# Low parts in two instructions, memory heads ahead, seams in another order, post norms by column halves

## The chip, the cores and the metric

One core of a Trainium2 chip runs the whole program in one launch. The metric is the device time of an execution in microseconds. The kernel before ran three times: 1194.78, 1198.9 and 1200.14 us, median 1198.9.

## What is computed

Two transformer blocks, one after the other, on 256 tokens of width 1024, all in float32. The first block: a norm, one wide projection that feeds three mixers (softmax attention with decay, a gated delta rule with convolution, stick-breaking attention), their gated sum through `w_out`, an attention to 256 memory tokens with normalised queries and keys, and a feed-forward of width 2816 with a convolution. The second block: a SwiGLU, a mixer of block attention and pooling, an attention to a second memory, and another SwiGLU, each with a norm before and after. Cut to the second block and its norm:

```python
def rmsnorm_2(x, g):
    r = lax.rsqrt(jnp.mean(x * x, axis=-1, keepdims=True) + RMS_EPS)
    return (x * r) * g
def second_block(x, mem, ...):
    x = x + 0.5 * rmsnorm_2(swiglu(rmsnorm_2(x, ffn1_pre_g), ...), ffn1_post_g)
    x = x + rmsnorm_2(mixer(rmsnorm_2(x, mix_pre_g)) @ w_out, mix_post_g)
    x = x + rmsnorm_2(attend(rmsnorm_2(x, xa_pre_g), rmsnorm_2(mem, mem_g)) @ wo, xa_post_g)
    x = x + 0.5 * rmsnorm_2(swiglu(rmsnorm_2(x, ffn2_pre_g), ...), ffn2_post_g)
```

## The kernel before, in words

**Weights in chunks.** All weights are cut into 178 chunks of 1 MB (128 partitions x 2048 columns of float32). SP fetches chunk c into `raw[c % 3]`. ScalarE rounds it to the matmul's type, the high part `whi` (step `hi`, line 1536), and VectorE subtracts, the low part `wlo` (step `lo`, line 1793). The activations are kept as a high and a low part too, and a product is three: high by high, high by low, low by high. `RING` is 3 and `LEAD` is 2: at the start of chunk c's product the parts of chunk c + 2 are put on their engines (`split`). SP's next fetch into a slot waits for that slot's `lo`, the next `hi` for the product that last read the slot.

**Kinds of chunks.** `W`, `A` and `S` give 256 output channels turned (channels on partitions), `V` gives half of the depth for 512 value channels, `O` is a branch's output, `R` gives two blocks of depth for token rows of 1024 columns. Each product is two steps, `mm(c, 0)` and `mm(c, 1)`, and, where side work is due, each of these is cut once more (`mma` is its first half, `quarter` and `hook`). For `W`, `V` and most `R` chunks the first part reads the first 1024 columns of the slot; for `A`, `O`, the last `R` chunk and the ones marked `by_token` both parts read all of it. `multiply` (from line 1170) issues the matmuls: lines 1196, 1203, 1206, 1214, 1217, 1224, 1233 and 1248 are those of the kinds.

**The planner.** `build_plan` writes the order of the steps of every engine ahead of time. It adds up rough durations (`ROUGH`) into a clock for each engine; chains of side work (delta rule, attention heads) wait in `side`, and `hook` places the next link of each where `fits` says that its input is ready in these sums, no more than `EARLY` ahead. `drain` places all that is left, one link after another, with nothing in between. `heads_of` makes the links of heads: scores `sc`, maximum `sm`, exponential `ex`, division `pn`, turn `pt` with its copy `pc`, values `pv`, the output's high part `oc` and low part `ol`. The four memory heads run in two lanes, 0 and 2, 1 and 3, with banks 4, 5 and 6, 7; queries and keys are normalised first (`hn_sq`, `hn_sum`, `hn_r`, `hn_mul`), the queries through bank 4 and the scratch of lane 0. All four waited for `mq1` and for the copy of the values `mv`.

**Seams.** A norm of x sits between two stages: squares `ns`, root `nr`, scaling `nd`, then TensorE turns x into blocks of 128 channels (`nt`, line 1262), ScalarE scales them into the high part (`nh`, 1565) and VectorE makes the low part (`nl`, 1808). Five groups of blocks go through four banks, so the fifth turn waits until the first group is read. `fill_and_turn` puts a chunk that doesn't need x under the norm, and then the turn; at `norm_xq`, `norm_ffn` and `ffn1_pre_g_2` the chunk's addition (line 2075) and the low part of the chunk after next follow behind the turn, in this order. At `mix_pre_g_2` and `xa_pre_g_2` the filling chunks are value chunks in plain `mm` calls, with their copy (line 1607) and low parts ahead of the turn.

**Post norms.** Behind the last token-row chunk of each stage of the second block (`post`): squares of the product from PSUM on ScalarE (`post1`, line 1768), product times gain on VectorE (`post0`, 2044), root (`post_r`), and x plus that times the root (`post2`, 2049), for each 128 tokens. `post0` waits for `post1`, which writes the same scratch. For `ffn2_pre_g_2` the order is by hand in `seam`: the first 128 tokens of the last two chunks are finished first, their post norm and norm run under the other tokens' products, and the turn (`nt2`, 1277), high (`nh2`, 1572) and low parts (`nl2`, 1814) are made for each 128 tokens; the first gate chunk is multiplied in the same two passes. At the very end SP writes the output in two transfers, one for each 128 tokens (line 1022).

## Time and profile before

| | |
|---|---|
| Median of three runs | 1198.9 us |
| The profiled execution | 1200.3 us |
| Its span, first to last instruction | 1198.6 us |
| Mean granted clock of TensorE | 0.992 |
| Instructions | 16754 |
| Read from HBM | 191.82 MB |

The span and every row further down are of one execution, which took 1200.3 us; 1.7 us of it lie around the span. PE is TensorE's matmuls, PEld its weight loads, DVE is VectorE, ACT ScalarE, POOL GpSimd, SPq SyncE's queue. A row of a timeline has the start in us, the length in us, engine, line and operation, what it writes <- reads with its shape, how many were merged, and in brackets the engine's idle time ahead of it with what ended it.

### The profile page before, as it was taken

How to read it: one execution, taken by the hardware profiler on the slowest of the kernel's cores; microseconds unless marked ns; L12 is line 12 of the kernel's file. 1: busy time of each engine (PE TensorE's matmuls, PEld its weight loads, DVE VectorE, ACT ScalarE, POOL GpSimd, SP SyncE). 2: the span in 40 equal slices, each digit the busy share in tenths (PEclk: the TensorE clock that was granted, in tenths of full speed). 3: DMA queues.
4: the chain of work that ended last, by engine and by line, in shares of the span. 5: the costliest groups of instructions: out<-in, count | busy, mean ns of one | idle time of the engine just before them, and what ended most of it. 6: DMA issues, size and time to landing. Idle time of an engine off the chain costs nothing.

```text
span 1198.6 us, 16754 instructions
## 1 busy us (share of the span) xinstructions
PE 1161.4 (97%) x6779; PEld 1011.5 (84%) x6779; DVE 811.4 (68%) x873; ACT 616.5 (51%) x788; POOL 82.2 (7%) x114
## 2 busy tenths in 40 slices
PE   6999999999999999999999999999999998999997
PEld 6877888888988789999888888888776887888886
DVE  5877655855778757878648777646776656777743
ACT  6656344533767655565536344436455546444432
POOL 8001200200000000000000000002700000000000
PEclk9999999999999999999999999999999998999999
DMA  7544323432655426555665565565533523665550
GB/s 252 169 158 148 106 71 106 137 109 71 214 201 170 153 86 213 178 177 181 211 206 173 179 188 198 178 208 195 182 136 111 186 83 124 208 198 186 186 200 36
DMA packets 144132, 193.95 MB, mean 162 GB/s; under 512 B 6136, under 2 KB 121208, under 8 KB 144056
## 3 DMA queue, kind: packets, MB, share of 16 engines
q1 hardware_dynamic: 142856, 188.43, 48.4%
q0 software_dynamic: 1200, 4.46, 1.0%
q8 instruction: 54, 0.88, 0.3%
q14 instruction: 22, 0.18, 0.0%
HBM read 191.82 MB, written 1.05 MB: 161 GB/s over the span
## 4 chain that ended last, share of the span: by engine, by line
PE 87%; DVE 6%; ACT 4%; issue 2%; DMA 1%; SPq 0%; ACTq 0%; DVEq 0%
PE banks L1214 24%; PE banks L1248 20%; PE banks L1196 14%; PE banks L1217 12%; PE banks L1233 4%; PE banks L1224 2%; DVE wlo L1793 2%; ACT whi L1536 2%; PE banks L1476 1%; PE banks L1307 1%; PE banks L1350 1%; PE banks L1396 1%; PE banks L1359 1%; DMA raw<-in_w_in 1%; PE banks L1436 1%
## 5 line engine op out<-in xcount | busy, mean ns | idle before, releaser
L1793 DVE TENSOR_TENSOR wlo<-raw,whi 128x2048 fp32r<-128x2048 f32 x178 | 407.4, 2293 | 180.8 <-ACT whi L1536 180.7
L1536 ACT ACTIVATE whi<-raw 128x2048 fp32r<-128x2048 f32 x178 | 339.2, 1910 | 174.4 <-PE banks L1248 87.4
L1214 PE MATMUL banks<-xhl,whi 128*128 128x512 f32 x1232 | 399.1, 405 | 3.4 <-DVE fq_ L2075 1.6
L1217 PEld LDWEIGHTS banks<-xhl,wlo 128*128 128x128 f32 x1232 | 232.8, 189 | 55.2
L1217 PE MATMUL banks<-xhl,wlo 128*128 128x256 f32 x1232 | 243.6, 279 | 0.0
L1214 PEld LDWEIGHTS banks<-xhl,whi 128*128 128x128 f32 x1232 | 190.1, 190 | 12.0 <-issue 6.8
L1196 PE MATMUL banks<-xhl,whi 128*128 128x256 f32 x912 | 167.0, 286 | 0.0
L1196 PEld LDWEIGHTS banks<-xhl,whi 128*128 128x128 f32 x912 | 143.9, 194 | 0.5 <-DVE xhl L1808 0.2
L1196 PE MATMUL banks<-xhl,wlo 128*128 128x256 f32 x456 | 129.9, 285 | 0.0
L1248 PE MATMUL banks<-whi,hh 128*128 128x512 f32 x264 | 102.7, 389 | 0.0
L1248 PE MATMUL banks<-wlo,hh 128*128 128x512 f32 x264 | 102.7, 389 | 0.0
L1248 PE MATMUL banks<-whi,hl 128*128 128x512 f32 x264 | 102.7, 389 | 0.0
L1196 PEld LDWEIGHTS banks<-xhl,wlo 128*128 128x128 f32 x456 | 88.5, 194 | 0.0
L1762 ACT ACTIVATE hh<-SG 128x512 fp32r<-128x512 f32 x33 | 20.9, 632 | 92.9 <-DVE SG L2091 92.9
L1248 PEld LDWEIGHTS banks<-whi,hl 128*128 128x128 f32 x264 | 49.6, 188 | 10.3
L1248 PEld LDWEIGHTS banks<-whi,hh 128*128 128x128 f32 x264 | 49.6, 188 | 10.3
L1248 PEld LDWEIGHTS banks<-wlo,hh 128*128 128x128 f32 x264 | 49.6, 188 | 10.0
L2087 DVE TENSOR_REDUCE CA<-banks 128x512 f32<-128x1024 f32 x22 | 26.9, 1225 | 24.7 <-PE banks L1217 24.7
L2057 DVE SCALAR_TENSOR_TENSOR CA<-banks,pcol,CA 128x255 f32<-128x255 f32 (+1 forms) x88 | 36.4, 476 | 8.4 <-ACT CA L1744 8.1
L2095 DVE TENSOR_TENSOR hl<-SG,hh 128x512 fp32r<-128x512 f32 x33 | 22.8, 692 | 27.3 <-ACT hh L1762 27.3
L1233 PE MATMUL banks<-whi,xhl 128*128 128x512 f32 x96 | 34.9, 418 | 0.0
L1102 POOL TENSOR_TENSOR gMs<-gM,lev 128x512 f32<-128x512 f32 x12 | 21.3, 1776 | 139.0 <-DVE gM L1901 96.6
(362 smaller groups left out, 1537.3 us busy)
## 6 DMA issues: line engine op xcount, KB each, us to landing
raw<-in_w_in SPq DMA_DIRECT2D x40, 1024.0 KB, 5.3
raw<-in_w_up SPq DMA_DIRECT2D x22, 1024.0 KB, 5.1
raw<-in_ffn_w_gate SPq DMA_DIRECT2D x22, 1024.0 KB, 5.3
raw<-in_ffn_w_up SPq DMA_DIRECT2D x22, 1024.0 KB, 5.3
raw<-in_ffn_w_down SPq DMA_DIRECT2D x22, 1024.0 KB, 5.0
raw<-in_w_down SPq DMA_DIRECT2D x11, 1024.0 KB, 5.0
raw<-in_w_out SPq DMA_DIRECT2D x8, 1024.0 KB, 5.1
raw<-in_xa_wkv SPq DMA_DIRECT2D x8, 1024.0 KB, 5.4
```

What stands on the lines that cost most here:

```text
L1102: pool.tensor_tensor(gMs[l % 2][:, :, :], gM[:, :, :], lev[:, l, :].unsqueeze(1).to_broadcast([P, NH, P]), ALU.mult).then_inc(pool_done, 1)
L1196: ins = pe.matmul(o, a[:, k, cols_], v[:, k, :], start=(k == 0 and i == 0), stop=(k == KD - 1 and i == 2))
L1214: pe.matmul(bank(b[m]), wh[:, k, m * P:(m + 1) * P], both[:, k, :, :].rearrange("p a t -> p (a t)"), start=(k == 0), stop=(k == KD - 1), s ...
L1217: ins = pe.matmul(bank(b[m])[:, 0:T], wl[:, k, m * P:(m + 1) * P], Xh[:, k, :], start=False, stop=(k == KD - 1), skip_group_check=True)
L1224: ins = pe.matmul(bank(b[part])[:, m * T:(m + 1) * T], a[:, k, o:o + P], v[:, k, :], start=(k == 0 and i == 0), stop=(k == NH - 1 and i == 2))
L1233: ins = pe.matmul(bank(b[t]), v[:, k, t * P:(t + 1) * P], a[:, kk, :], start=(k == 0 and i == 0), stop=(k == KD - 1 and i == 2))
L1248: ins = pe.matmul(bank(b[2 * t + nb]), v[:, k, t * P:(t + 1) * P], a[:, kk, nb * 512:(nb + 1) * 512], start=(ch["first"] and kk == 0 and i ...
L1536: act.activation(whi[c % RING][:, :], raw[c % RING][:, :], ACT.Copy).then_inc(act_done, 1)
L1793: dve.tensor_tensor(wlo[c % RING][:, :], raw[c % RING][:, :], whi[c % RING][:, :], ALU.subtract).then_inc(dve_done, 1)
L2057: ins = dve.scalar_tensor_tensor(d, bank(chunks[c]["banks"][0])[:, m * T:(m + 1) * T - s], pcolumn("ffn_conv", (2 - s) * 2 * KF + a * KF + ...
L2087: dve.tensor_reduce(mat(CA[i % 2][:, 1, :]), halves(c), AX_X, ALU.add).then_inc(dve_done, 1)
L2095: dve.tensor_tensor(hl[:, 2 * i:2 * i + 2, :], mat(SG[i % 2]), hh[:, 2 * i:2 * i + 2, :], ALU.subtract).then_inc(dve_done, 1)
```

## The change

The low part of each chunk is made by two instructions of 1024 columns, one right behind the other. A product's first part waits for the first, its second for the second; kinds `A` and `O`, the last token-row chunk and chunks by token (`whole_low`) wait for both. The planner's cost of `lo` becomes 1.2 for each.

The chains of the memory heads are offered to the hooks one chunk pair sooner, ahead of the two value chunks. Heads 0 and 1 wait for `mq0`, 2 and 3 for `mq1`; only head 1's scores wait for the values' copy; head 0's turn waits for `mq1`. The queries' norm uses bank 5 and a part of `xv_`.

In `fill_and_turn` the low part goes ahead of the addition, and it is used for `mix_pre_g_2` and `xa_pre_g_2` too, with the copy behind the low part. The post norms behind `xa_wo_2` and `ffn2_w_down_2` work on halves of 512 columns, each from its half of the product; the sum of squares of the first half goes in as the bias of the root. `seam` has a new order, with its norm by halves too. The output leaves in four transfers.

```diff
-ROUGH = {"lo": 2.29, "hi": 1.92, ...
+ROUGH = {"lo": 1.2, "hi": 1.92, ...
@@ Plan.add
         elif name == "hi" and ("mm", args[0] - RING, 1) in self.ended:
-            behind = max(self.ended["mm", args[0] - RING, 1], self.ended["lo", args[0] - RING] + 5.8)
+            behind = max(self.ended["mm", args[0] - RING, 1], self.ended["lo", args[0] - RING, 1] + 5.8)
         elif engine == "pe" and name in ("mm", "mma"):
-            behind = self.ended["lo", args[0]]
+            behind = self.ended["lo", args[0], 1 if self.whole_low(args[0]) else args[1]]
+    def whole_low(self, c):
+        ch = self.chunks[c]
+        return ch["kind"] in "AO" or ch["by_token"] or ch.get("last", False)
@@ build_plan, input_of
+        if name == "sc" and args == ["mem", 1]:
+            return pl.ended.get(("copy", max(c for c, ch in enumerate(chunks) if ch.get("to") == "mv")), 1e9)
+        if name == "sc" and args[0] == "mem" or name == "pt" and args == ["mem", 0]:
+            return pl.ended.get(("hn_mul", "mq1" if name == "pt" else f"mq{args[1] // 2}"), 1e9)
@@ split
             pl.add("act", "hi", c)
-            pl.add("dve", "lo", c)
+            low(c)
+    def low(c):
+        for q in range(2):
+            if c < n and ("lo", c, q) not in pl.number:
+                pl.add("dve", "lo", c, q)
@@ mm
         quarter(c, 0)
+        if halved(c):
+            post_half(c, 0, 0)
         pl.add("pe", "mm", c, 0)
...
+        elif halved(c):
+            post_half(c, 0, 1)
...
-        elif ev == "vcopy":
+        elif ev == "vcopy" and not keep:
...
+    def halved(c):
+        return chunks[c]["name"] in ("xa_wo_2", "ffn2_w_down_2") and chunks[c]["last"]
+    def post_half(c, t, h):
+        pl.add("act", "post1", c, t, h)
+        pl.add("dve", "post0", c, t, h)
+        if h == 0:
+            pl.add("dve", "post_e", c, t)
+        else:
+            pl.add("act", "post_r", c, t)
+            pl.add("dve", "post2", c, t, 0)
+            pl.add("dve", "post2", c, t, 1)
+    def root(name, t):
+        pl.add("act", "nr", name, t)
+        for h in range(2):
+            pl.add("dve", "nd", name, t, h)
@@ seam
-        split(c + LEAD)
-        pl.add("pe", "mm", c, 0)
-        pl.add("pe", "mm", last_, 0)
-        pl.add("act", "post1", last_, 0)
-        pl.add("dve", "post0", last_, 0)
-        pl.add("act", "post_r", last_, 0)
-        pl.add("dve", "post2", last_, 0)
-        pl.add("pe", "mm", c, 1)
-        pl.add("act", "hi", last_ + LEAD)
-        norm_scale(name, 0)
-        pl.add("pe", "mm", last_, 1)
...
-        pl.add("act", "post1", last_, 1)
-        pl.add("dve", "post0", last_, 1)
-        for j in groups:
-            pl.add("pe", "nt2", name, 0, j)
-        halves_of(0, 0, 1)
-        pl.add("act", "post_r", last_, 1)
-        pl.add("dve", "post2", last_, 1)
-        halves_of(0, 2, 3, 4)
-        norm_scale(name, 1)
-        pl.add("dve", "lo", last_ + LEAD)
+        def part_of(t, h):
+            pl.add("pe", "mma" if h == 0 else "mm", last_, t)
+            pl.quartered.add((last_, t))
+        split(c + LEAD)
+        pl.add("pe", "mm", c, 0)
+        part_of(0, 0)
+        post_half(last_, 0, 0)
+        part_of(0, 1)
+        post_half(last_, 0, 1)
+        pl.add("pe", "mm", c, 1)
+        pl.add("act", "ns", name, 0, 0)
+        pl.add("dve", "ns_e", name, 0)
+        pl.add("act", "ns", name, 0, 1)
+        root(name, 0)
+        part_of(1, 0)
+        post_half(last_, 1, 0)
+        part_of(1, 1)
...
         for j in groups:
             pl.add("pe", "nt2", name, 0, j)
+        halves_of(0, 0)
+        post_half(last_, 1, 1)
+        pl.add("act", "nh2", name, 0, 1)
+        pl.add("act", "ns", name, 1, 0)
+        for k in turns(name)[1]:
+            pl.add("dve", "nl2", name, 0, k)
+        pl.add("dve", "ns_e", name, 1)
+        halves_of(0, 2)
+        pl.add("act", "ns", name, 1, 1)
+        pl.add("act", "nh2", name, 0, 3)
+        pl.add("act", "nr", name, 1)
+        for k in turns(name)[3]:
+            pl.add("dve", "nl2", name, 0, k)
+        for h in range(2):
+            pl.add("dve", "nd", name, 1, h)
+        halves_of(0, 4)
+        pl.add("act", "hi", last_ + LEAD)
...
         pl.add("pe", "mm", gate_, 0)
         for j in groups:
             pl.add("pe", "nt2", name, 1, j)
         halves_of(1, *groups)
+        low(last_ + LEAD)
@@ fill_and_turn
         norm_turn(name, base)
-        pl.add("dve", "add", c)
-        pl.add("dve", "lo", c + LEAD)
+        low(c + LEAD)
+        if chunks[c]["evac"] == "vcopy":
+            pl.add("act", "copy", c)
+        else:
+            pl.add("dve", "add", c)
@@ build_plan, the order of the chunks
     finished[id(turn_m2)] = max(pl.ended["nd", "mem_g_2", 1], pl.ended["add", c - 1])
+    for lane in range(2):
+        side.append(heads_of("mem", [lane, lane + 2]))
     mm(c)
     mm(c + 1)
     c += 2
-    drain()
-    for lane in range(2):
-        side.append(heads_of("mem", [lane, lane + 2]))
+    while turn_m2:
+        place(turn_m2.pop(0)[0])
...
-    mm(c + 1)
+    fill_and_turn(c + 1, "mix_pre_g_2", 4)
     c += 2
-    norm_turn("mix_pre_g_2", 4)
...
-    mm(c + 1)
+    fill_and_turn(c + 1, "xa_pre_g_2", 0)
     c += 2
-    norm_turn("xa_pre_g_2", 0)
@@ the kernel
-            HN[f"mq{i}"] = (mq_[:, s, :], S2[0], PT2[0], 4, pcolumn("mq_norm"), 1.0 / HD, 1.0, None)
+            HN[f"mq{i}"] = (mq_[:, s, :], xv_[:, 0, 0:512], xv_[:, 0, 512:D], 5, pcolumn("mq_norm"), 1.0 / HD, 1.0, None)
-                    sp.wait_ge(dve_done, at("lo", c - RING))
+                    sp.wait_ge(dve_done, at("lo", c - RING, 1))
             for t in range(NT):
-                sp.wait_ge(dve_done, at("post2", len(chunks) - 1, t))
-                sp.dma_start(out[t * P:(t + 1) * P, :], x[:, t, :]).then_inc(out_done, 16)
+                for h in range(2):
+                    s = half_of(h)
+                    sp.wait_ge(dve_done, at("post2", len(chunks) - 1, t, h))
+                    sp.dma_start(out[t * P:(t + 1) * P, s], x[:, t, s]).then_inc(out_done, 16)
@@ multiply
+                if 0 in quarters:
+                    if part == 0 or not plan.whole_low(c):
+                        pe.wait_ge(dve_done, at("lo", c, 1 if plan.whole_low(c) else part))
                 if part == 0 and 0 in quarters:
-                    pe.wait_ge(dve_done, at("lo", c))
@@ sc, pt
-                    pe.wait_ge(dve_done, at("hn_mul", "mq1"))
-                    pe.wait_ge(act_done, at("copy", chunk_of("mv", None)))
+                    pe.wait_ge(dve_done, at("hn_mul", f"mq{h // 2}"))
+                    if h == 1:
+                        pe.wait_ge(act_done, at("copy", chunk_of("mv", None)))
...
+                if kind == "mem" and h == 0:
+                    pe.wait_ge(dve_done, at("hn_mul", "mq1"))
@@ lo
-            def lo(c):
+            def lo(c, q):
                 dve.wait_ge(act_done, at("hi", c))
-                dve.tensor_tensor(wlo[c % RING][:, :], raw[c % RING][:, :], whi[c % RING][:, :], ALU.subtract).then_inc(dve_done, 1)
+                o = slice(1024 * q, 1024 * q + 1024)
+                dve.tensor_tensor(wlo[c % RING][:, o], raw[c % RING][:, o], whi[c % RING][:, o], ALU.subtract).then_inc(dve_done, 1)
@@ the first half's sum becomes the bias of the root over the second's
+            def first_half(t):
+                dve.tensor_scalar(eb[:, t:t + 1], ms[:, t:t + 1], 1.0 / D, EPS, ALU.mult, ALU.add).then_inc(dve_done, 1)
```

## Rows read from the trace of the kernel before

**Rows 1.** The page, busy time by engine, and the clock in 40 slices.

```profile
PE 1161.4 (97%) x6779; PEld 1011.5 (84%) x6779; DVE 811.4 (68%) x873; ACT 616.5 (51%) x788; POOL 82.2 (7%) x114
...
PEclk9999999999999999999999999999999998999999
```

**Rows 2.** Busy time by stretch: PE, PEld, DVE, ACT, POOL, then granted clock.

```profile
0.00:15.00 15.00, 4.83 (x21) 4.06 (x22) 5.74 (x9) 9.48 (x17) 12.16 (x29) 1.00 0.91 294
422.10:425.50 3.40, 3.40 (x12) 2.73 (x11) 2.29 (x1) 0.70 (x2) 0.00 (x0) 0.50 0.02 5
1002.30:1009.20 6.90, 6.62 (x31) 6.65 (x32) 6.18 (x11) 3.57 (x11) 0.64 (x2) 0.51 0.23 77
```

**Rows 3.** End of the chain; the output among the DMA issues, last: landing.

```profile
1191.73 1.12 ACT xs L1768 x2
...
1192.94 1.24 DVE xs L2044
...
1194.20 1.29 DVE x_tok L2049
...
out<-x_tok SPq DMA_DIRECT2D x2, 512.0 KB, 2.7
```

**Rows 4.** Waits of TensorE: engine line <- releaser: us in total, times, longest.

```profile
PE banks L1214 <- DVE wlo L1793: 0.8, 1, 0.8
```

**Rows 5.** Timeline, ScalarE and TensorE around the memory heads.

```profile
399.78 1.09 ACT L1607 ACTIVATE mv_<-banks 128x512 f32<-128x512 f32 x2
...
401.53 1.13 PE L1430 MATMUL banks<-mk_,mq_ 128*128 128x256 f32 x4 [0.77 <-DVE mq_ L1880]
...
418.68 0.63 PE L1456 MATMUL banks<-ident,S 128*128 128x128 f32 x4 [1.07 <-DVE y2l L1985]
421.03 0.47 PE L1248 MATMUL banks<-whi,y2h 128*128 128x512 f32 x1 [1.73 <-DVE y2l L1985]
```

**Rows 6.** Timeline from 641 to 645 us: start, length, engine, what, idle before.

```profile
641.20 1.23 DVE L2075 TENSOR_REDUCE xk_<-banks 128x512 f32<-128x1024 f32 x1
642.34 4.49 DVE L1793 TENSOR_TENSOR wlo<-raw,whi 128x2048 fp32r<-128x2048 f32 x2
...
644.68 0.74 PE L1214 MATMUL banks<-xhl,whi 128*128 128x512 f32 x2 [0.78 <-DVE wlo L1793]
```

**Rows 7.** Timeline, ScalarE and TensorE at the turn ahead of the mixer.

```profile
832.86 1.09 ACT L1607 ACTIVATE xv_<-banks 128x512 f32<-128x512 f32 x2 [1.50 <-PE banks L1233]
...
835.12 0.41 PE L1262 MATMUL banks<-ident,xs 128*128 128x128 f32 x2 [0.83 <-DVE xhl L1808]
```

**Rows 8.** Timeline, TensorE and VectorE at the turn ahead of memory attention.

```profile
936.65 0.41 PE L1262 MATMUL banks<-ident,xs 128*128 128x128 f32 x2 [0.82 <-DVE xhl L1808]
...
943.27 1.22 DVE L2075 TENSOR_REDUCE qk_<-banks 128x512 f32<-128x1024 f32 x1
```

**Rows 9.** Timeline of the last seam, three engines.

```profile
996.05 1.92 ACT L1536 ACTIVATE whi<-raw 128x2048 fp32r<-128x2048 f32 x1 [1.05 <-PE banks L1248]
...
1000.62 0.98 PE L1277 MATMUL banks<-ident,xs 128*128 128x128 f32 x7 [1.95 <-DVE xs L1803]
...
1000.95 1.23 DVE L2044 SCALAR_TENSOR_TENSOR xs<-banks,gain 128x1024 f32<-128x1024 f32 x1 [0.39 <-PE banks L1277]
...
1002.58 0.45 PE L1277 MATMUL banks<-ident,xs 128*128 128x128 f32 x1 [0.97 <-DVE xhl L1814]
...
1010.74 0.48 PE L1203 MATMUL banks<-xhl,whi 128*128 128x256 f32 x2
```

**Rows 10.** VectorE's groups of instructions: xcount | busy us, mean ns of one.

```profile
L1793 DVE TENSOR_TENSOR wlo<-raw,whi 128x2048 fp32r<-128x2048 f32 x178 | 407.4, 2293 | 180.8 <-ACT whi L1536 180.7
...
L2091 DVE TENSOR_TENSOR SG<-SG,CA 128x512 f32<-128x512 f32 x33 | 22.8, 692 | 1.1
```

**Rows 11.** Timeline, TensorE at the end of the side chains.

```profile
292.02 1.02 PE L1307 MATMUL banks<-gKb,ones 128*128 128x512 f32 x2
...
298.45 0.28 PE L1224 MATMUL banks<-ybh,whi 128*128 128x256 f32 x1
```

More of the change, by code:

```diff
@@ L65, in param_columns @@
     return col, first, n
[L68 removed]
+ROUGH = {"lo": 1.2, "hi": 1.92, "add": 1.23, "copy": 1.2, "cv_mul": 0.9, "cv_add": 2.2, "cv_silu": 0.63, "gated": 1.35,
          "ns": 1.06, "nr": 0.42, "nd": 0.66, "nh": 0.95, "nl": 0.48, "resid": 1.22, "gsig": 4.6, "gzs": 4.0, "tables": 1.5,
@@ L352, in mm @@
                 pl.take(("mm", c, t), ch["banks"][2 * t:2 * t + 2], end[chunks[e]["evac"]][:1] + (e, t))
+                for h in range(2) if halved(e) else ():
+                    pl.bank_read[ch["banks"][2 * t + h]] = ("post0", e, t, h)
         for s in late:
@@ L368, in mm @@
         quarter(c, 1)
+        if halved(c):
+            post_half(c, 1, 0)
         pl.add("pe", "mm", c, 1)
@@ L408, in quarter @@
     def quarter(c, part):
-        if side:
+        if side or halved(c):
             pl.add("pe", "mma", c, part)
@@ L747, in two_blocks_kernel @@
         ms = small[:, 32:34]
+        msb = small[:, 54:56]
+        eb = small[:, 56:58]
         rn = small[:, 34:36]
@@ L1548, in ns @@
                     act.wait_ge(dve_done, at("resid", LAST_ROWS[name], t))
+                elif h is not None:
+                    act.wait_ge(dve_done, at("post2", LAST_ROWS[name], t, h))
                 elif name in LAST_ROWS:
@@ L1553, in ns, with root @@
                     act.wait_ge(pe_done, at("nt", NORM_BEFORE[name], len(turns(NORM_BEFORE[name])) - 1))
-                act.activation(junk[:, t, :], src[:, t, :], ACT.Square, accum_out=ms[:, t:t + 1]).then_inc(act_done, 1)
+                s = half_of(h)
+                act.activation(junk[:, t, s], src[:, t, s], ACT.Square, accum_out=(msb if h else ms)[:, t:t + 1]).then_inc(act_done, 1)
             def nr(name, t):
                 act.wait_ge(pool_done, at("consts"))
-                link(act.activation(rn[:, t:t + 1], ms[:, t:t + 1], ACT.Ln, bias=eps, scale=1.0 / D))
+                if ("ns_e", name, t) in plan.number:
+                    act.wait_ge(dve_done, at("ns_e", name, t))
+                    root(t, msb, eb[:, t:t + 1])
+                else:
+                    root(t, ms, eps)
+            def root(t, sum_, bias):
+                link(act.activation(rn[:, t:t + 1], sum_[:, t:t + 1], ACT.Ln, bias=bias, scale=1.0 / D))
                 act.activation(rn[:, t:t + 1], rn[:, t:t + 1], ACT.Exp, scale=-0.5).then_inc(act_done, 1)
```

57 lines of the change are left out of this document (37 added, 20 removed).

## The prediction

> **What bounds the kernel now.** Start with the share of busy time: TensorE 1161.4 us of a span of 1198.6, VectorE 811.4 [rows 1]. TensorE sets the time, so only what keeps it idle, or slow, can be won. 37.2 us are idle. The two ends hold 17.1 of them: 10.2 of the first 15 us, in which TensorE is busy for 4.83 [rows 2], and the 6.9 us from the last squares, at 1191.73, to the end of the span [rows 3]. So 20 us are left for the whole middle.
>
> Next, the waits of TensorE: who ended them. The low part of the weights stands there with one wait of 0.8 us [rows 4]. So the first words of the change's description (a split low part, products that wait per part) can give 0.8 us directly, whatever they look like; the other waits belong to norms and heads. I looked for each one's place in the timeline: 0.77, 1.07 and 1.73 us around the memory heads [rows 5], 0.78 after a filled seam [rows 6], 0.83 and 0.82 in two unfilled ones [rows 7, 8], 1.95 and 0.97 at the last seam [rows 9].
>
> Third, the clock. It is granted in full nearly everywhere, but after such stops it falls: 0.50 for 3.4 us behind the memory heads, where two stops of 1.07 and 1.73 us stand ahead of it, and for 6.9 us behind the last seam [rows 2]. That is 1.2 GHz for 2.4 GHz: TensorE was busy all of the 3.4 us and did the work of 1.7, and at the seam it lost up to 3.4 us. A stop can cost as much again behind it as in it.
>
> **The change part by part.** All against the profiled execution, 1200.3 us (its span is 1198.6); the median of the runs is 1198.9, 1.4 less.
>
> *Two instructions for each low part.* 178 instructions of 2.293 us become 356 of half the columns. A row of 128x512 takes 0.692 [rows 10]; the line through both gives 1.04 ns a column and 0.16 us fixed, so 1.22 us for 1024 columns, 2.45 a pair. Two adjoining whole ones took 4.49, not 4.59 [rows 6], so a successor hides about 0.1. A pair costs 2.35 to 2.45, and VectorE gets 10 to 28 us more work. It is idle for 387 us of the span, so that lies beside TensorE's work, except where VectorE is waited for: at the start, where the first low part stands ahead of the first norm's halves: **0.1 us lost**. Without that cover (a stretch in which TensorE waits for VectorE link by link) it would cost 0.1 us for each chunk, as in the chains of the first 300 us.
>
> The Trainium skill (VectorE: DVE Perf Modes, "The TRN2 errata — SBUF-src ops pay a fixed extra latency per instruction") speaks against cutting an instruction up: it says that small tiles pay a fixed latency each, and that (N+151)/0.96 holds for an fp32 tensor_tensor. By that a pair costs 2.45 us, the trace's upper end, and the sum stays as it is.
>
> *The filled seams.* At 644.68 TensorE waits 0.78 us for a low part that stands behind an addition of 1.23 us [rows 6]. The change puts the low part first and lets the chunk start on its first half, 1.2 + 1.1 = 2.3 us sooner: **0.8 us won**, surely; next late is nothing, as the addition's banks are wanted a chunk later. The weight slot is freed sooner too, so SP's next transfer starts sooner.
>
> *Two more seams filled.* Ahead of ffn1's and the mixer's turn ScalarE copies a value chunk for 1.09 us before it can scale the first turned block; TensorE's last turn waits 0.83 us for that block's bank, 0.82 at the other [rows 7, 8]. The change puts copy and low part behind the turn: the first block comes 1.1 us sooner, more than the wait. But the low part of the chunk after next is made behind the turn, about 5 us later, and what stands behind it on VectorE with it: SP's reload of its slot, and the addition (1.22 us) for which the first memory-attention scores wait at the second seam [rows 8]. Those scores then want it earlier and get it later; a later hook may take them. **1.25 us won**: 1.65 less 0.4 (ends: 0.3 lost, 1.65 won).
>
> *Memory heads sooner.* The scores of head 0 wait for mq0 alone, and are placed during the value chunk; heads 1 and 3 still wait for the values' copy, which ends at 400.87 [rows 5]. To free its bank, the queries' norm goes from bank 4 to 5, so head 0's turn must wait for mq1 there. Head 0's chain starts about 3 us sooner and leaves heads 1 and 3 less company on VectorE. The stops of 0.77, 1.07 and 1.73 us, 3.57 together, lie one behind the other in these chains, and nothing but order makes them. I take 2.5 of them, since the second lane can't start sooner, and the 1.7 us of the slow clock, which came after the two longest: **4.2 us won** (ends: 1 lost, if the next thing late is the second lane's last output; 5.3 won).
>
> *The last seam.* TensorE ends the token rows at 998.7 and waits 1.95 us, to 1000.62: the squares of the new x stood behind a high part of 1.92 us at 996.05 [rows 9]. The change moves that high part behind the second token's norm, and does the post norm in column halves, each from the moment that its half of the product is there. From the durations (a half square about 0.75 with its read-out, a half on VectorE about 0.7) the first token's scaled x is ready at about 998.4: no wait. The fifth turn waited 0.97 us behind a post norm of 1.23 at 1000.95; now the first block's low half goes ahead of it. But the other blocks are now woven between the second token's post norm steps: by the same durations the first block is there at about 999.5, the next two at 1002.4, then 1003.2, 1004.6 and 1005.7. So the gate's first pass starts near 999.7 instead of 1002.7 (behind the last turn at 1002.58) and stops on the way, longest about 2 us; with those stops I keep one slow stretch of 3.4 us. The second pass started at 1010.74 [rows 9]; I get 1008.3: **2.4 us won** (ends: 0.5, if the clock stays low as long as now; 5, if it never falls). The up chunk's high and low parts get late there, to about 1011.5, just as the chunk wants them; its wait per half is the cover.
>
> *The tail.* Now 1.12 + 1.24 + 1.29 us lie one behind the other [rows 3]. In halves: square 0.7, post norm 0.7, residual 0.7 and 0.7, so 2.8, and 0.8 less; the first halves are done while TensorE works. Each output transfer carries half as much, and four issues stand on SP for two: I put 0.2 more. **1.0 us won** (0.3 to 1.5). The Trainium skill (DMA: Bandwidth & Descriptors, "Anatomy of one DMA — SWDGE (gpsimd) path") gives 2.0 us and 1 us for each 436 KB, for the software path: half as many bytes would bring 0.6 us, and the sum 0.4 more. No row has an output of half the size; the whole ones took 2.7 [rows 3].
>
> *The planned order.* The planner's cost of a low part goes from 2.29 to 2 x 1.2. The links of the side chains in the first 300 us are placed by such sums, so some move by a quarter chunk. No row tells which way: 0, bounds 2.5 us on both sides (as long as two of the stops seen there or one slow stretch).
>
> Sum: -0.1 + 0.8 + 1.25 + 4.2 + 2.4 + 1.0 = 9.55 us. 1200.3 becomes 1190.7; as the median stands 1.4 lower, **1189.4**.
>
> **The rivals.**
> *The stops move instead of going* (nearly the same). The second lane of memory heads ends as late as before, the second new seam gives back what it won, the last seam's slow clock lasts. For it: heads 1 and 3 still start with the copy; my weaving leaves stops. Then 0.5 + 0.8 + 0.5 + 0.7 + 0.8 + 1.0 is 4.3 us: 1194.6.
> *No slow stretches.* All stops but the ends go and with them the slow clock: 5.3 + 0.8 + 1.65 + 5 + 1.3 - 0.1 is 14: 1185. Against it: eight blocks have to pass one after the other at the last seam.
> *The delta-rule chain runs out of cover* (slower). Its last sum is placed at 292.02, and the branch stage starts at 298.45 [rows 11]; what is not placed by then is drained with nothing beside it. With dearer low parts in the planner's sum it may come later. A link then shows its whole latency, some 3 us (square, a sum of 1.02, root, a multiplication of 0.69), and every second or so a slow stretch of 1.7. Up to 6 us of delay cost nothing; it decides against the whole when about four links fall out, 12 + 3.5 us: 1205. Against it: the sum changes by 0.11 us a chunk.
> *It doesn't do what it says:* a wait per part that frees no product. True of all but one wait [rows 4]; it is in the sum.
>
> **How the numbers follow.** About 0.5%, 6 us, is what a measurement of this kernel tells from no change. My forecast, 1187 to 1192.5, gets 0.57; no slow stretches 0.13; moved stops 0.25; the chain 0.05. Faster by over 0.5% (below 1192.9): 0.70; within: 0.25; slower: 0.05. The range goes from 1183.5 to 1196: it takes in both neighbours and the bounds of the planned order.
>
> **What would show it.** TensorE's waits: no 0.8 for the low part, no stop of over 1 us between 400 and 425, none for the last turn at the two seams. The clock: full behind the memory heads, and at most one stretch of 3.4 us at the last seam. Low parts: 356 of about 1.22 us, VectorE near 830. From the last matmul to the end 6 us, not 6.9. Wrong: a drained chain near 300, or a new wait for a low part behind the new seams.

## The result and the profile after

The changed kernel took 1214.93 us (median of four executions, 1214.03 to 1218.53), the kernel before, on the same chip, 1197.18 (1194.78 to 1200.14): a ratio of 1.0149, 95% interval 1.0131 to 1.0167. The change makes the kernel 1.5% slower, where the forecast was 0.8% faster, and the result lies outside the range, on the side that had a chance of 0.05. The profiled execution took 1215.8 us; its span is 1214.0. Two of experiment 6's twelve executions (1235.55 us in a slow state of the chip, and 5435.85) are left out of its ratio.

From the page of the kernel after: span, busy time by engine, the clock in 40 slices, and the low parts' group.

```profile
span 1214.0 us, 16999 instructions
...
PE 1165.3 (96%) x6779; PEld 1015.3 (84%) x6779; DVE 827.4 (68%) x1067; ACT 617.9 (51%) x800; POOL 75.1 (6%) x114
...
PEclk9999999998699999999999999999999998999999
...
L1885 DVE TENSOR_TENSOR wlo<-raw,whi 128x1024 fp32r<-128x1024 f32 x356 | 421.5, 1227 | 178.6 <-ACT whi L1612 178.6
```

Beside [rows 1] TensorE has as many matmuls, and only 4 us more busy time, but the span is 15.4 us longer: TensorE stands idle. The clock's row has an 8 and a 6 in its tenth and eleventh slice of 30.35 us, 273 to 334 us; that is where to look. The low part has its two instructions at 1.227 us.

The waits of TensorE, kernel after: engine, what it wrote and line <- releaser, us in total, times, longest.

```profile
PE banks L1380 <- DVE gq_ L1988: 3.2, 1, 3.2
PE banks L1423 <- DVE gY L2024: 2.9, 2, 1.6
...
PE banks L1532 <- DVE y2l L2089: 1.9, 1, 1.9
PE banks L1530 <- DVE S L2076: 1.8, 1, 1.8
PE banks L1469 <- DVE gMs L2039: 1.7, 2, 0.9
PE banks L1456 <- DVE gq_ L2034: 1.6, 1, 1.6
...
PE banks L1380 <- DVE gS L2045: 1.4, 1, 1.4
PE banks L1456 <- DVE gS L2045: 1.4, 1, 1.4
...
PE banks L1287 <- DVE xk_ L2181: 0.9, 1, 0.9
```

`wlo` is gone, as forecast, with its 0.8 us [rows 4]; `xk_`, 0.9, is new and stands in its place. And a family has grown: everything with a `g` in front (`gq_`, `gY`, `gMs`, `gS`) is the delta rule's chain. Before, its waits were 1.3 us for `gY` in five short ones and 0.3 for `gU`. The timeline of TensorE shows how its links stand:

```profile
283.52 1.16 PE L1432 MATMUL banks<-gU,gX 128*128 128x128 f32 x8 [0.75 <-ACT gU L1738]
285.56 1.16 PE L1438 MATMUL banks<-gVb,gY 128*128 128x128 f32 x8 [0.88 <-DVE gY L2024]
286.55 1.06 PE L1440 MATMUL banks<-gY,gKb 128*128 128x128 f32 x8
288.45 1.15 PE L1446 MATMUL banks<-gdec,picks 4*128 4x128 f32 x8 [0.84 <-DVE gM L2029]
291.24 1.34 PE L1456 MATMUL banks<-gS,gU 128*64 128x128 f32 x8 [1.63 <-DVE gq_ L2034]
...
301.23 1.94 PE L1456 MATMUL banks<-gS,gU 128*64 128x128 f32 x8 [1.38 <-DVE gS L2045]
...
311.84 2.05 PE L1380 MATMUL banks<-gKb,ones 128*128 128x512 f32 x2 [1.38 <-DVE gS L2045]
317.11 2.04 PE L1380 MATMUL banks<-gKb,ones 128*128 128x512 f32 x2 [3.23 <-DVE gq_ L1988]
318.17 1.20 PE L1297 MATMUL banks<-ybh,whi 128*128 128x256 f32 x1
```

From 276.2 us, where the last weight product of the projection ends, to 318.17 no product of weights runs. The links of the chain stand one behind the other, each waits for VectorE or ScalarE, and the same two sums that took 1.02 us [rows 11] take 2.05 at half the clock. The branch stage begins at 318.17 instead of 298.45 [rows 11], 19.7 us late. From there on the stages of the kernel after are shorter than before's by 4.3 us together (the span is 15.4 longer, not 19.7); 1.7 of this is the slow stretch at 422 us [rows 2], which this execution doesn't have.

Busy time by stretch (PE, PEld, DVE, ACT, POOL, granted clock), kernel after, first the slow stretch, then from 244 us to the branches:

```profile
291.90:322.60 30.70, 23.02 (x82) 17.94 (x81) 6.50 (x14) 6.63 (x11) 0.00 (x0) 0.50 0.00 1
...
244.00:318.10 74.10, 57.62 (x330) 49.05 (x329) 32.54 (x44) 16.97 (x20) 6.10 (x4) 0.82 0.21 72
```

The same view of the kernel before, from 244 us to its branches:

```profile
244.00:298.40 54.40, 53.73 (x328) 46.29 (x327) 30.44 (x34) 17.03 (x18) 1.30 (x1) 0.97 0.30 98
```

The same work (330 and 328 matmul groups) took 74.1 us for 54.4. TensorE's idle time there went from 0.7 to 16.5 us, and its busy time grew by 3.9, the half clock's share.

### The profile page after: what moved, and what is told of

It is laid out like the page before. It is cut to its first block, busy times and chain, and to the rows that moved or that the text cites. A ratio compares the mean times of both kernels' runs of the same rounds, so it can differ in the third digit from the quotient of the medians.

```text
span 1214.0 us, 16999 instructions
## 1 busy us (share of the span) xinstructions
PE 1165.3 (96%) x6779; PEld 1015.3 (84%) x6779; DVE 827.4 (68%) x1067; ACT 617.9 (51%) x800; POOL 75.1 (6%) x114
## 4 chain that ended last, share of the span: by engine, by line
PE 88%; DVE 7%; ACT 3%; issue 2%; DMA 1%; SPq 0%; DVEq 0%; ACTq 0%
PE banks L1287 24%; PE banks L1321 19%; PE banks L1269 13%; PE banks L1290 12%; PE banks L1306 5%; PE banks L1297 2%; DVE wlo L1885 2%; PE banks L1552 1%; PE banks L1380 1%; PE banks L1469 1%; ACT whi L1612 1%; PE banks L1335 1%; PE banks L1423 1%; PE banks L1432 1%; DMA raw<-in_w_in 1%
## 5 line engine op out<-in xcount | busy, mean ns | idle before, releaser
L1885 DVE TENSOR_TENSOR wlo<-raw,whi 128x1024 fp32r<-128x1024 f32 x356 | 421.5, 1227 | 178.6 <-ACT whi L1612 178.6
L2201 DVE TENSOR_TENSOR hl<-SG,hh 128x512 fp32r<-128x512 f32 x33 | 22.9, 692 | 27.3 <-ACT hh L1848 27.3
```

Of the source, the lines that this page charges most:

```text
L1885: dve.tensor_tensor(wlo[c % RING][:, o], raw[c % RING][:, o], whi[c % RING][:, o], ALU.subtract).then_inc(dve_done, 1)
L2201: dve.tensor_tensor(hl[:, 2 * i:2 * i + 2, :], mat(SG[i % 2]), hh[:, 2 * i:2 * i + 2, :], ALU.subtract).then_inc(dve_done, 1)
```

## The experiments

"Before" beside each is the kernel before in the same series on the same chip: median 1198.43 us (25 executions) for the first four experiments, 1198.13 (32) for the next four, 1198.01 (22) for the last four. The three series ran on three chips, so experiments of different series are compared by their ratios, or by the length of a stage in their profiles. Theory P: the planner's number alone (2.29 to 2 x 1.2) puts the delta rule's links so late that they are drained; the kernel's other edits are small gains. Rival Q: the second instruction for each low part, or its waits, makes the engines late.

**1. The change with the planner's old cost.**

```diff
-ROUGH = {"lo": 1.2,
+ROUGH = {"lo": 1.145,
```

> The changed kernel with one number changed: the planner's cost of a low part 1.145 instead of 1.2, so that a pair sums to the 2.29 of before. Theory (the planned order is the whole loss): the delta-rule chain is placed in full before the branch stage, no slow stretch of 30 us near 300, the branch stage starts near 298.5 us as before, and the other parts' gains show: 1191 to 1194 us against 1197 to 1199 for the kernel before. Rival (the two instructions and the other new waits cost the time themselves, for example through VectorE's 16 us more): it stays above 1208 us.

Measured: 1196.89 us (10 executions), ratio 0.9989 [0.9973, 1.0005]. One constant of the planner is worth some 18 us. That is above the 1191 to 1194 expected: P holds for the large loss, but of the 9.5 us forecast for the rest 1.5 are left, and the interval takes in none at all.

**2. The kernel before with a dearer low part in the planner, and nothing else changed.**

```diff
-ROUGH = {"lo": 2.29,
+ROUGH = {"lo": 2.46,
```

> The kernel before, with one number changed: the planner's cost of a low part 2.46 instead of 2.29. No instruction is added or removed, only the places of side links among the products move. Theory (the planned order alone can lose this much): a drained chain ahead of the branch stage, a long stretch at the low clock, 12 to 22 us slower, 1210 to 1220 us. Rival (the drain needs the split or the other parts): within 3 us of before.

Measured: 1224.91 us, 1.0203 [1.0176, 1.0231], more than the 1210 to 1220 us expected; the clock is at half for 27.3 us from 293.7. Q falls as the cause of the large loss: no instruction was cut here, and the loss is larger than the change's.

**3. The same with 2.40**, the sum that the change's planner uses.

> The kernel before with the planner's cost of a low part 2.4, the sum that the change gives it. If a dearer low part by itself pushes the chain out, 8 us or more slower. If it is a matter of where single links fall (the order is sensitive, not steadily worse), the chain still ends before the branch stage and the time is within 3 us of before: 1195 to 1201 us.

Measured: 1199.12 us, 0.9996 [0.9981, 1.0012]. The same sum that costs the changed kernel 18 us costs the kernel before nothing. The loss isn't proportional to the number; it hangs on where each link happens to fall.

One line of code tells the rest: L1471, the state's update. Shown for each kernel are its shortest, median and longest duration in ns, and its first and last start in us.

Kernel after:

```profile
L1471 PE MATMUL banks<-gMs,gKt x32: 272/395/579, 207.0 to 310.0; 64*128 64x128 f32 x32
```

Experiment 1:

```profile
L1471 PE MATMUL banks<-gMs,gKt x32: 272/272/373, 182.3 to 283.1; 64*128 64x128 f32 x32
```

The kernel before, and below it experiment 2 (there it is L1398):

```profile
L1398 PE MATMUL banks<-gMs,gKt x32: 272/272/419, 183.7 to 282.5; 64*128 64x128 f32 x32
```

```profile
L1398 PE MATMUL banks<-gMs,gKt x32: 272/395/579, 212.9 to 311.1; 64*128 64x128 f32 x32
```

The chain is not late only at its end; it is 25 us late already at its first update, 100 us earlier. The planner is arithmetic on constants, so its two orders can be written out side by side. The chunk behind whose product a link is placed, and its planned time:

```
link                        1.145: chunk, us      1.2: chunk, us
queries' sum  gq1           10    69.2            10    69.4
keys' sum     gk1           11    79.4            12    80.4
decay         g_dec 0       12    86.0            13    89.1
turn          g_turn 0      14   102.7            16   111.3
inverse       l_u 0 1       15   114.3            18   125.4
inverse       l_u 0 3       17   130.1            20   147.3
inverse       l_u 0 5       18   147.4            23   176.5
update        r_o 0 0       20   173.9            25   197.2
update        r_o 1 1       30   267.1            32   288.0
last sum      go1           31   276.4            32   295.4
```

At the end of chunk 11 the keys' sum is ready at 78.44 with 1.145, and the hook takes what is ready by 78.45: it fits by 0.01 us. With 1.2 it is ready at 78.88 and the limit is 78.67: the link goes to the next hook. The link behind it misses another, and so on: four to five chunks of lag from chunk 18 on.

The same working answers experiment 3. With 2.40 the sum is ready at 78.88 too, but there the planner lets a product wait for the whole low part; TensorE's clock in the plan stands later, the limit is 79.83, and the link fits. With 2.46 it is ready at 81.16 against 80.90 and misses. With its own 2.29 the kernel before has 78.44 against 79.50. So theory P's "alone" is too strong: the planner's new rule for the wait cut the margin at this hook from 1.06 us to 0.01, and the number took the rest. Nor does the plan grow steadily with the number: TensorE's planned sum for the change is 1197.5 us with 1.17, 1188.3 with 1.18, 1194.2 with 1.19 and 1202.4 with 1.2.

The projection's side work ends with chunk 32, whose product holds no more hooks than another, and the rest is drained: in the trace 11 stops of 0.75 to 3.23 us, 14.1 together, between 276 and 318 us.

**4. The kernel before with the split low part and the waits per part, its planned order untouched.** (The cost is 1.145 for each half, which gives the same order step by step.)

```diff
-            def lo(c):
+            def lo(c, q):
                 dve.wait_ge(act_done, at("hi", c))
-                dve.tensor_tensor(wlo[c % RING][:, :], ...
+                dve.tensor_tensor(wlo[c % RING][:, o], ...
@@ multiply
+                    if part == 0 or not plan.whole_low(c):
+                        pe.wait_ge(dve_done, at("lo", c, 1 if plan.whole_low(c) else part))
```

> The kernel before with the split alone: low parts in two instructions of 1024 columns, waits per part, planner's cost 1.145 each; no other part of the change. Theory: 0.3 us lost at the start, 0.8 us won at the filled seam (the addition still stands ahead of the low part there), in all 0 to 1 us faster, about 1197 to 1198.5 us. Rival (a finer low part frees much): 3 us or more faster. Rival (its overhead costs on the path in the chains): 2 us or more slower.

Measured: 1201.3 us, 1.0029 [1.0013, 1.0045]. The stop of 0.78 us [rows 6] is gone and the stage around it is 1.06 us shorter (189.91 for 190.97 us between the down projections), as forecast; yet the kernel lost 2.9 us, as the rival with a cost on the chains' path had it. Cutting the instruction costs about 4 us somewhere else. VectorE's timeline, kernel before:

```profile
218.17 2.38 DVE L1793 TENSOR_TENSOR wlo<-raw,whi 128x2048 fp32r<-128x2048 f32 x1
220.59 1.12 DVE L1907 TENSOR_SCALAR gVb<-banks,gcols 128x128 f32<-128x128 f32 x4
```

and GpSimd's:

```profile
217.13 4.58 POOL L1102 TENSOR_TENSOR gMs<-gM,lev 128x512 f32<-128x512 f32 x2 [15.54 <-DVE gM L1901]
```

The same place in experiment 4: GpSimd, VectorE, TensorE.

```profile
218.25 3.50 POOL L1112 TENSOR_TENSOR gMs<-gM,lev 128x512 f32<-128x512 f32 x2 [15.49 <-DVE gM L1913]
...
219.29 3.55 DVE L1805 TENSOR_TENSOR wlo<-raw,whi 128x1024 fp32r<-128x1024 f32 x2
222.87 1.13 DVE L1919 TENSOR_SCALAR gVb<-banks,gcols 128x128 f32<-128x128 f32 x4
...
224.14 0.63 PE L1359 MATMUL banks<-ident,gMs 128*128 128x128 f32 x4 [1.21 <-DVE gVb L1919]
```

Whole, the low part took 2.38 us and GpSimd's two masks 4.58: GpSimd stood. Cut, GpSimd takes 3.50 and the pair 3.55 in place of 2.36: its second half took 2.30, so VectorE stood. GpSimd got in between the halves, and the next link behind it on VectorE was 1.2 us late for TensorE. In this kernel it happens at 112.7, 141.8 and 219.3 us (pairs of 3.56, 3.44 and 3.55). The Trainium skill (SBUF — State Buffer, "SBUF: two separate sides") says that a VectorE instruction with two inputs in SBUF and a GpSimd instruction that reads SBUF take a shared port pair as an exclusive lock, and that the later one stands until the other is done; the trace agrees, with 3.55 for 2.36 us.

**5. Experiment 1 with the first 38 low parts (to the end of the branches, at 313.6 us) in one instruction.**

```diff
-                o = slice(1024 * q, 1024 * q + 1024)
+                o = slice(1024 * q, 1024 * q + 1024) if c >= WHOLE else slice(0, 2048)
```

> e1_cost_1145 with the first 38 low parts (all up to the end of the branches) in one instruction again, the later ones in two; the order of all steps is the same. Theory (a cut low part lets a GpSimd mask of 1.3 to 2.2 us in between, and its second half stands until GpSimd is done): the pairs of 3.4 to 3.6 us near 110, 140 and 219 become 2.3 to 2.4, the stop of 1.2 us near 222 goes, and the start is 0.2 to 0.4 us sooner; 1.5 to 3 us faster than e1, near 1194.5. Rival (the split's 0.3 per cent is slow clock or chance): the same as e1 within 0.7 us.

Measured: 1193.85 us, 0.9966 [0.9953, 0.9978]; 0.0023 less than experiment 1's ratio, about 2.8 us, with the same order. The long pairs and the stop of 1.2 us near 222 are gone. The stretch from 15 to 290 us (busy time as above: PE, PEld, DVE, ACT, POOL, clock) of the kernel before, experiment 4 and experiment 5:

```profile
15.00:290.00 275.00, 269.32 (x1675) 236.00 (x1675) 188.34 (x246) 136.41 (x186) 36.13 (x33) 0.99 0.40 125
```

```profile
15.00:290.00 275.00, 267.95 (x1677) 235.31 (x1677) 193.45 (x280) 136.37 (x186) 30.07 (x32) 0.99 0.40 125
```

```profile
15.00:290.00 275.00, 269.31 (x1692) 235.50 (x1691) 191.25 (x250) 137.26 (x187) 35.72 (x32) 0.99 0.40 127
```

TensorE is idle in it for 5.7, 7.1 and 5.7 us: 1.4 us of the split's price are stops here, and with whole instructions they are gone. With 0.3 to 0.4 at the start that is 1.8 of some 3; no row shows the rest. So it is shown that the halves cost time here. That it is the lock, and not the 0.07 us that each pair takes beyond a whole low part (2.36 for 2.29, some 2.5 us of VectorE over 35 of them), rests on the three long pairs, behind two of which experiment 4 has stops of 0.45 and 1.21 us that neither neighbour has, and on experiment 12.

**6. Experiment 5 with the addition ahead of the low part again, in all three seams filled by additions.**

```diff
-        low(c + LEAD)
         if chunks[c]["evac"] == "vcopy":
+            low(c + LEAD)
             pl.add("act", "copy", c)
         else:
             pl.add("dve", "add", c)
+            low(c + LEAD)
```

> e5_whole_early with the addition ahead of the low part again in the three seams that are filled by a product with an addition. Theory (the new wait of 0.94 us near 642 is for the banks that the late addition reads, and the split alone had removed the old one): no stop there, the ffn1 stage 1.0 us shorter (190.0 us from one down projection to the next for 191.1); 0.5 to 1.5 us faster than e5. Rival (the order doesn't matter): the stop stays.

Measured: 1197.43 us, ratio 0.999 [0.9976, 1.0005]: not 0.5 to 1.5 us faster than experiment 5 but 3.6 slower, with two places that move in opposite ways. At the feed-forward seams the addition first is better: the stage is 189.91 us for 191.08. VectorE and TensorE of the kernel after show why.

```profile
659.81 2.35 DVE L1885 TENSOR_TENSOR wlo<-raw,whi 128x1024 fp32r<-128x1024 f32 x2
662.20 1.23 DVE L2181 TENSOR_REDUCE xk_<-banks 128x512 f32<-128x1024 f32 x1
```

```profile
663.57 0.70 PE L1287 MATMUL banks<-xhl,whi 128*128 128x512 f32 x2 [0.94 <-DVE xk_ L2181]
```

The product behind the turn writes the banks that the addition reads: the wait changed its name, from the low part's 0.78 to the addition's 0.94. At the norm of the memory queries it is the other way round: from the first product of the first memory's keys to the first of `w_mo` the stage takes 63.74 us with the addition first and 62.02 with the low part first (63.55 before); with the addition first the kernel before's stops of 0.38, 0.51 and 0.77 us between 374 and 402 us are partly back, and two of 2.08 and 2.15 stand in the heads. The last 2 us of its 63.74 are at half the clock, so up to 1.0 of the difference is the clock's.

**7. Experiment 1 with the old last seam.** (Post norm of `xa_wo_2` whole again, and the order of `seam` as before: the diff of the section on the change, turned around.)

> e1_cost_1145 with the last seam's order of before (whole post norm and norm of each 128 tokens behind xa_wo_2), the rest of the change kept. If the new seam is worth what I took for it, 2.4 us slower than e1. By the profiles (155.5 to 156.7 us from the last attention rows to the last down projection against 156.2 to 156.9) it is worth 0.3 to 0.7: the same as e1 within 1 us.

Measured: 1197.12 us, 0.9987 [0.997, 1.0004], experiment 1's 0.9989. By the medians the new seam is worth nothing that these runs can tell. Of the timeline of the kernel after:

```profile
1015.45 1.06 PE L1350 MATMUL banks<-ident,xs 128*128 128x128 f32 x7
...
1017.12 0.30 PE L1350 MATMUL banks<-ident,xs 128*128 128x128 f32 x1 [0.61 <-DVE xhl L1918]
...
1019.59 0.79 PE L1276 MATMUL banks<-xhl,whi 128*128 128x256 f32 x2 [1.59 <-DVE xhl L1918]
...
1027.01 0.48 PE L1276 MATMUL banks<-xhl,whi 128*128 128x256 f32 x2
```

The stop ahead of the turn (1.95 us [rows 9]) is gone as worked out, and the fifth turn's is 0.61 for 0.97; but the second block's low part then comes 1.59 us late, and in this execution the clock is at half for 6.8 us behind it, as before. It isn't always so: of the nine profiles with the new seam three have 6.8 us at half there, four 3.4 and two none, while of the five with the old one four have 6.8 and one 3.4. From the first row of `xa_wo_2` to the first of the last down projection it is 156.6 to 156.7 us, 155.4 to 155.5 and 154.9 with the new seam; with the old one 156.9 to 157.3 and 156.2. So the seam gains 0.3 to 0.7 us at an equal clock. Whether it makes slow stretches rarer, one profile a kernel can't tell. From the end of the token rows to the second pass it is 11.6 us (1015.4 to 1027.0) for 12.0.

**8. Experiment 1 with the memory heads offered as late as before.**

```diff
-    for lane in range(2):
-        side.append(heads_of("mem", [lane, lane + 2]))
     mm(c)
     mm(c + 1)
     c += 2
-    while turn_m2:
-        place(turn_m2.pop(0)[0])
+    drain()
+    for lane in range(2):
+        side.append(heads_of("mem", [lane, lane + 2]))
```

> e1_cost_1145 with the memory heads offered one chunk pair later, behind a drain, as before the change. By my forecast 4.2 us slower than e1. By the profile (value and memory stages 62.0 us for 63.6, the stops of 1.93 and 1.26 us ahead of the output rows still there) 1.0 to 1.8 us slower.

Measured: 1197.06 us, 0.9986 [0.9969, 1.0004]; memory keys to `w_mo` 62.02 us, and 62.03 in experiment 1. Offering the heads sooner brings nothing at all. It does start the chain sooner: head 0's maximum comes 45.7 us behind the first product of the memory keys in experiment 1, and 47.4 here, both times behind a low part of 2.36 us. But the stage ends no sooner. The kernel after:

```profile
422.82 2.36 DVE L1885 TENSOR_TENSOR wlo<-raw,whi 128x1024 fp32r<-128x1024 f32 x2 [2.76 <-ACT whi L1612]
425.21 0.69 DVE L2065 TENSOR_REDUCE small<-banks 128x2 f32<-128x512 f32 x1
```

```profile
438.84 0.63 PE L1532 MATMUL banks<-ident,S 128*128 128x128 f32 x4 [1.93 <-DVE y2l L2089]
439.31 1.03 PE L1552 MATMUL banks<-PT,mv_ 128*128 128x256 f32 x4
441.60 0.47 PE L1321 MATMUL banks<-whi,y2h 128*128 128x512 f32 x1 [1.26 <-DVE y2l L2089]
```

1.93 and 1.26 stand for 1.07 and 1.73 [rows 5]; in experiment 8 the last two are 0.39 and 1.89. The slow stretch behind them doesn't follow from them each time: experiments 2 and 3, with the order of the kernel before and its stops in this stage, have the next stage at 148.2 us where the profile of before has 149.8, without it; experiment 4 has it.

**9. Experiment 5 with the addition first at the two feed-forward seams only.**

> e5_whole_early with the addition ahead of the low part at the seams of norm_ffn and ffn1_pre_g_2 alone; norm_xq keeps the low part first. e6 had the stop near 640 gone (1.2 us), but lost 1.7 us around the memory keys, where its order of before was back, and two stops of over 2 us with 6.8 us of low clock. Theory (two seams want different orders): the stop of 0.94 goes, nothing is lost at the keys, 1 us faster than e5 (about 1193). Rival (e6's loss was chance): no difference between them at the keys, e9 like e6 (1197).

Measured: 1193.36 us, 0.996 [0.9946, 0.9974]: 0.0006 less than experiment 5's ratio, which the intervals can't tell from nothing. Its profile has the feed-forward stage at 189.92 us and no wait for the addition; the heads' stage stays at 62.00. By the stages both gains are had, as each place has the order that frees what is wanted first.

**10. Experiment 5 without the two seams that the change fills anew.**

```diff
-    fill_and_turn(c + 1, "mix_pre_g_2", 4)
+    mm(c + 1)
     c += 2
+    norm_turn("mix_pre_g_2", 4)
@@ and the same at xa_pre_g_2
```

> e5_whole_early without the two new filled seams (mix_pre_g_2 and xa_pre_g_2 as before the change). By my forecast their part is worth 1.25 us. By the profiles the two stops of 0.83 and 0.82 come back, and the stop at the first block-attention division falls from 1.82 to 1.25: about 0.9 to 1.1 us slower than e5; a slow stretch of 1.7 can hide it in the median.

Measured: 1195.45 us, 0.9982 [0.9966, 0.9997], 0.0016 or 1.9 us more than experiment 5, which the intervals alone don't settle; the stages, 0.3 us at the first seam and 1.15 at the second, do. This part of the change does what was forecast.

**11. The change with 1.18**, about what the second half of a pair takes.

> The changed kernel with the planner's cost of a low part 1.18 for 1.2, which is what a half takes in the trace (a pair 2.36). If the loss of the change grows steadily with the cost, most of it stays: 1208 us or more. If it is where single links fall (theory), the chain ends nearly in time with this one: within 4 us of e1, 1195 to 1201 us.

Measured: 1203.43 us, 1.0049 [1.0031, 1.0067]. It fell between the bounds of both theories: a better estimate of the instruction is no cure, but nor is the chain drained whole. The state's updates:

```profile
L1471 PE MATMUL banks<-gMs,gKt x32: 272/272/373, 192.6 to 297.3; 64*128 64x128 f32 x32
```

In the plan the keys' sum misses its hook here too (78.72 against 78.59), and fewer links miss theirs behind it. The chain is ten us late at its first update instead of 25, the branches begin at 305.2, and the stops of 1.64, 1.46 and 1.84 us (at 224, 236 and 303) with two more slow stretches are what it costs. So the price of the order takes values between, here about 7 us by the ratios of this and experiment 1; P in the form "drained or not" was too coarse.

**12. Experiment 9 with whole low parts also for chunks 124 to 134**, where GpSimd pools windows for the mixer.

> e9 with the low parts of chunks 124 to 134 in one instruction as well, where GpSimd makes the pooling windows. Theory (the cut lets GpSimd in): the pair of 2.9 us ahead of the first block-attention maximum becomes 2.3 to 2.4, and the stop of 1.8 us at the first division falls to 1.2 to 1.3; about 0.6 us faster than e9. Rival (that stop has another cause, the low part that the filled seam made late): it stays at 1.8.

Measured: 1192.52 us, 0.9949 [0.993, 0.9969]. The stop in the mixer's heads, 1.20 before and 1.82 in experiments 1 and 9, is 1.32; the rival expected it to stay at 1.8. It takes both edits to make it long: in experiment 10, with halves but without the filled seam, it is 1.25. This is the fastest version, 5.5 us (0.5%) ahead of the kernel before; its lead of 0.8 over experiment 9 lies within the intervals. By the two ratios it is 2% faster than the change. TensorE's waits in it:

```profile
PE banks L1540 <- DVE S L2086: 1.3, 1, 1.3
...
PE banks L1433 <- DVE gY L2034: 1.3, 5, 0.5
```

## Why the prediction was wrong

**The planned order** (forecast 0, ends 2.5 us either way; measured 18 us lost). This is the step that failed, and it decides the result. It was taken for nothing without either order being written out. Two sentences carried it: "some move by a quarter chunk. No row tells which way", and, of the third rival, "Against it: the sum changes by 0.11 us a chunk". The second takes the effect to be of the size of its cause. `fits` is a threshold, and a link that misses it waits for the next hook, which makes the next link miss it too: 0.11 us a chunk became five chunks. It also left out the planner's other edit, that a product waits for half a low part, which moves every hook's limit. Rival three named the mechanism, the place and the kind of loss (late chain, drained links, slow clock, a later start of the branches); its size was worked out for four links where 11 stops came, and its chance of 0.05 was a judgement about a number that is plain arithmetic. The planner's own sum for TensorE is 1186.6 us for the kernel before, 1202.4 for the change, 1186.7 for experiment 1 and 1207.4 for experiment 2; the differences of 15.8 and 20.8 stand beside 18 and 26.5 measured. Experiment 11 (planned 1188.3, measured 5.4 us above the kernel before) isn't seen in it, and why the plan and the chip part there stays open.

**Two instructions for each low part** (forecast 0.1 lost; measured about 3, in experiments 4 and 5). A pair takes 2.36 us, at the lower end of what was worked out. The estimate of 2.45 from the formula of the Trainium skill (VectorE: DVE Perf Modes, "The TRN2 errata — SBUF-src ops pay a fixed extra latency per instruction") is 0.09 above it. The working asked what the cut costs VectorE and hid it in VectorE's idle time; it didn't ask who else wants to go between the halves. [Rows 2] had GpSimd busy for 12 of the first 15 us, and the low parts beside GpSimd's work could have been looked up. The start lost 0.2 to 0.4 us rather than 0.1.

**The filled seams** (0.8 won; measured nothing). "Next late is nothing, as the addition's banks are wanted a chunk later" was wrong: the product behind the turn wants them, and waits 0.94 us for 0.78. What the new order of low part and addition did bring was at a seam that the prediction left out, the norm of the memory queries: about 1.5 us (63.55 to 62.03; back at 63.74 in experiment 6).

**Two more seams filled** (1.25 won; measured 1.5 in the stages). Right, in size too: the stops of 0.83 and 0.82 [rows 7, 8] are gone, and the memory-attention scores still wait, 0.26 us for 0.46. The first seam gained only 0.3, since it made the stop in the mixer's heads 0.6 longer.

**Memory heads sooner** (4.2 won; measured 0). Wrong in its mechanism: the chain's end doesn't hang on when head 0 starts. Its maximum came 1.7 us sooner and the stage took 62.0 us all the same. The rival of the moved stops said so ("The second lane of memory heads ends as late as before"); which link holds the end stays open. The 1.7 us for the slow stretch was read as an effect of the stops; experiments 2 and 3 have the stops without it.

**The last seam** (2.4 won; measured 0.3 to 0.7 at an equal clock). The first turn came without a stop, and a stop of about 2 us on the way was forecast, 1.59 found. The second pass started 11.6 us behind the token rows, where 9.6 were worked out (998.7 to 1008.3) and 12.0 stood before. Part of this is the slow clock, of which 3.4 us were put in: 6.8 came in this execution, 3.4 in four other profiles and none in two. The term's lower end was 0.5, and that is about what happened.

**The tail** (1.0 won; measured 0.83). The last matmul's start to the end is 6.49 us for 7.32, the same in every kernel that has the edit. (The 6.9 of the prediction's last lines runs from the last squares, not from the last matmul.) The whole outputs landed in 2.7 us [rows 3], the halves in 2.1:

```profile
out<-x_tok SPq DMA_DIRECT2D x4, 256.0 KB, 2.1
```

Put together, without the planner's number: tail 0.8, memory queries' seam 1.5, two new seams 1.5 (with the mixer's heads, whose stop grew from 1.20 to 1.82), last seam 0.4, split 3.0 lost, which is 1.2 won; experiment 1 had 1.5. Several of these are known to no better than 1 us, so that they meet so closely is partly luck.

## What to carry to other kernels

A scheduler with thresholds and constants is part of the kernel: when a constant changes, write out both orders and compare where each chain's links fall, before any duration is argued about, for a change of a few hundredths of a microsecond can move a chain by whole tiles. Before an instruction is cut so that its first half is ready sooner, ask who is waiting to get in between the halves, and which waiter is next when a wait is removed. Gains found in one kernel should be tried place by place: here the same swap gained 1.5 us at one seam and lost at another, and whole low parts beside GpSimd's work with halves elsewhere beat halves everywhere. Whole ones everywhere, with the rest of the change, weren't run.

## What the runs showed of the hardware

A VectorE subtraction with both inputs in SBUF that adjoins GpSimd's masks took 2.30 us for 1024 columns instead of 1.22, and 2.38 for 2048 when it had begun first.

In the drained chain TensorE had 23.0 us busy in 30.7 and the clock stayed at 0.50 for all of it; the dense products had begun at 318.2 when it rose at 322.6, in experiment 2 at 319.3 when it rose at 321.0. The chain's own matmuls ran at twice their length in it: two sums took 1.02 us at the full clock [rows 11] and 2.05 in it.

Executions of one kernel differ by whole slow stretches: of the kernel before those with a mean clock of 0.995 lie at 1194.6 to 1198.1 us, those with 0.992 at 1198.0 to 1200.5. Each stretch of 3.4 us costs 1.7 of TensorE's work, and behind the same stops it comes in one profile and not in another (the memory heads in experiments 4, 2 and 3; the new last seam with 6.8, 3.4 or none); one profile can't price it.
